# Differential-attention norm of a two-layer decoder: row sums taken with tokens on partitions, then spread back by a product with diagonals

## The reference, cut to what matters

```python
o_b = causal_block_attention(qd, kd, vd, 1.0 / math.sqrt(DIFF_HD),
                             lambda p: p[:, :, 0] - lam * p[:, :, 1])
o_b = rms_norm(o_b, diff_subln_g) * (1.0 - lambda_init)      # over the 128 channels of a head
y_b = o_b.transpose(0, 2, 1, 3).reshape(bsz, s, DIFF_HEADS * DIFF_VD) @ w_out_diff
```

## Time and profile before

| what | value |
|---|---|
| time, median of 3 runs | 1041.09 us (1040.82 to 1041.31) |
| profiled execution | 1040.82 us, of which 1039.0 us from first to last instruction |
| PE matrix products busy | 986.8 us, 95% of the span |
| DVE busy | 741.0 us, 71% |
| ACT busy | 525.2 us, 51% |
| mean granted clock of TensorE | 0.989 of full |

### The profile page before, as it was taken

One profiled execution on the slowest core, in us unless ns is written; L12 is line 12 of the kernel. 1 busy time (PEld: TensorE's weight loads), 2 busy tenths in 40 slices (PEclk: granted clock), 3 DMA queues, 4 the chain that ended last, 5 costly groups with the idle time before them and its releaser, 6 DMA issues.

```text
span 1039.0 us, 20424 instructions
## 1 busy us (share of the span) xinstructions
PE 986.8 (95%) x7817; PEld 917.9 (88%) x7817; DVE 741.0 (71%) x1113; ACT 525.2 (51%) x735; POOL 18.0 (2%) x23
## 2 busy tenths in 40 slices
PE   3699999999999999999999999999999999999997
PEld 2498899889888999989898999888998989999997
DVE  2448889986485787876345698999558577888733
ACT  2655355547444555653345544654734465555532
POOL 5000000000000000000000000000000000000001
PEclk9899999999999999999999999999999999999999
DMA  9865545546594555966763545553678635555551
GB/s 306 293 203 166 174 149 187 173 139 233 203 353 153 161 164 176 350 244 238 275 203 93 161 138 172 187 165 132 204 243 310 216 124 163 177 188 163 185 181 42
DMA packets 138952, 202.25 MB, mean 195 GB/s; under 512 B 3416, under 2 KB 114148, under 8 KB 138852
## 3 DMA queue, kind: packets, MB, share of 16 engines
q1 hardware_dynamic: 138501, 200.68, 57.6%
q10 hardware_dynamic: 351, 0.21, 0.1%
HBM read 199.83 MB, written 1.05 MB: 193 GB/s over the span
## 4 chain that ended last, share of the span: by engine, by line
PE 73%; DVE 13%; issue 7%; ACT 2%; DMA 2%; SPq 2%; DVEq 0%; ACTq 0%
PE PB L1282 16%; PE PB L1284 15%; PE PB L1283 15%; DVE wL L866 5%; DVE buf L953 2%; PE SC L1282 2%; PE MI L1233 2%; PE SC L1283 2%; PE SC L1284 2%; DMA raw<-in_w_in 2%; DVE rdev L1011 1%; PE PB L1305 1%; PE ST L1335 1%; DVE cb L1099 1%; PE TR L1284 1%
## 5 line engine op out<-in xcount | busy, mean ns | idle before, releaser
L866 DVE TENSOR_TENSOR wL<-raw,wH 128x2048 fp32r<-128x2048 f32 (+3 forms) x152 | 322.8, 2125 | 120.1 <-ACT wH L610 118.5
L1282 PE MATMUL PB<-hH,wH 128*128 128x256 f32 x1376 | 398.0, 289 | 7.6 <-DVE wL L866 7.5
L1284 PE MATMUL PB<-hH,wL 128*128 128x256 f32 x1376 | 390.6, 284 | 0.0
L1283 PE MATMUL PB<-hL,wH 128*128 128x256 f32 x1376 | 390.5, 284 | 0.0
L610 ACT ACTIVATE wH<-raw 128x2048 fp32r<-128x2048 f32 (+3 forms) x152 | 268.3, 1782 | 123.9 <-DMA raw<-in_w_down 57.4
L1282 PEld LDWEIGHTS PB<-hH,wH 128*128 128x128 f32 x1376 | 265.1, 193 | 22.7 <-issue 12.3
L1283 PEld LDWEIGHTS PB<-hL,wH 128*128 128x128 f32 x1376 | 265.2, 193 | 0.9 <-issue 0.7
L1284 PEld LDWEIGHTS PB<-hH,wL 128*128 128x128 f32 x1376 | 265.1, 193 | 0.0
L953 DVE SCALAR_TENSOR_TENSOR buf<-G,vec,buf 128x256 f32<-128x256 f32 x240 | 98.0, 477 | 0.3
L1305 PE MATMUL PB<-hH,wH 128*128 128x256 f32 x192 | 56.9, 297 | 15.2 <-DVE hL L883 12.3
L1099 DVE SCALAR_TENSOR_TENSOR cb<-PB,vec,cb 128x255 f32<-128x255 f32 (+1 forms) x88 | 36.3, 476 | 32.2 <-ACT cb L757 32.2
(11 more groups left out here) (257 smaller groups left out, 1695.6 us busy)
## 6 DMA issues: line engine op xcount, KB each, us to landing
raw<-in_w_in SPq DMA_DIRECT2D x48, 1024.0 KB, 5.4
raw<-in_w_up SPq DMA_DIRECT2D x44, 1024.0 KB, 5.1
ada<-in_ada_w SPq DMA_DIRECT2D x40, 1024.0 KB, 7.6
raw<-in_w_down SPq DMA_DIRECT2D x22, 1024.0 KB, 4.9
ada_pre<-in_ada_w SPq DMA_DIRECT2D x8, 1024.0 KB, 11.8
raw<-in_w_o SPq DMA_DIRECT2D x8, 1024.0 KB, 8.3
raw<-in_w_out_diff SPq DMA_DIRECT2D x4, 1024.0 KB, 5.0
raw<-in_w_out_conv SPq DMA_DIRECT2D x4, 1024.0 KB, 7.4
```

The source lines that it names most:

```text
L866: dve.tensor_tensor(wL[s][:, 0:size], raw[s][:, 0:size], wH[s][:, 0:size].bitcast(F32), ALU.subtract).then_inc(w_lo[s], 1)
L1282: pe.matmul(out, a, xh(k), start=first and k == 0, stop=False, skip_group_check=True)
L1283: pe.matmul(out, a, xl(k), start=False, stop=False, skip_group_check=True)
L1284: ins = pe.matmul(out, b, xh(k), start=False, stop=last and k == kt - 1, skip_group_check=True)
```

## The change

The sums of squares are taken with the roles of the operands exchanged: the squares are the stationary operand (four blocks of 128 channels x 128 tokens), two columns of ones the moving one. The result has tokens on partitions and only 8 columns in `ST`, in 4 pairs of equal columns. Root (ACT) and reciprocal (DVE) work on 8 columns in a new tile `rtok`. DVE then multiplies the identity, repeated four times, by the four columns, which gives four 128 x 128 diagonal matrices in `rdev`; PE multiplies ones with these 512 columns (`SPREAD0` behind chunk 18, `SPREAD1` behind chunk 23), and the product has the reciprocal roots in all partitions. The scaling of `oB` reads it straight from the bank and stands one step later than before (19 and 24), as do `oBH` (ACT, 20 and 25) and `oBL` (DVE, 21 and 26). The other uses of `ST` only have their counts moved by two.

```diff
-ST_USES = ["N1", "LAT", "SUB0", "SUB1", "LNS", "LNQ", "N2"]
+ST_USES = ["N1", "LAT", "SUB0", "SPREAD0", "SUB1", "SPREAD1", "LNS", "LNQ", "N2"]
-STATS_AT = {3: "LAT", 17: "SUB0", 22: "SUB1", 26: "LNS", 28: "LNQ"}
+STATS_AT = {3: "LAT", 17: "SUB0", 18: "SPREAD0", 22: "SUB1", 23: "SPREAD1", 26: "LNS", 28: "LNQ"}
...
+        rtok = sb("rtok", [P, 8])
...
                 elif use in ("SUB0", "SUB1"):
                     st_done(l, use)
-                    act.activation(rdev[:, :], ST[:, :], ACT.Sqrt, bias=eps[:, :], scale=1.0 / P).then_inc(st_read, 1)
+                    act.activation(rtok[:, :], ST[:, 0:8], ACT.Sqrt, bias=eps[:, :], scale=1.0 / P).then_inc(st_read, 1)
...
-                if n in (19, 24):
-                    i = (19, 24).index(n)
-                    act.wait_ge(sub_y, l * 2 + i + 1)
+                if n in (20, 25):
+                    i = (20, 25).index(n)
+                    act.wait_ge(st_read, FREE + l * len(ST_USES) + 4 + 2 * i)
                     act.activation(oBH[:, 2 * i:2 * i + 2, :].rearrange("p k t -> p (k t)"),
                                    oBq[:, 2 * i:2 * i + 2, :].rearrange("p k t -> p (k t)"), ACT.Copy).then_inc(sub_hi, 1)
...
                 if n in (18, 23):
 
                     i = (18, 23).index(n)
-                    dve.wait_ge(st_read, FREE + l * len(ST_USES) + 3 + i)
-                    link(dve.reciprocal(rdev[:, :], rdev[:, :]))
+                    dve.wait_ge(st_read, FREE + l * len(ST_USES) + 3 + 2 * i)
+                    link(dve.reciprocal(rtok[:, :], rtok[:, :]))
+                    dve.tensor_tensor(rdev[:, :].rearrange("p (j t) -> p j t", j=4),
+                                      ident.unsqueeze(1).broadcast_to([P, 4, P]),
+                                      rtok[:, 0:8:2].unsqueeze(2).broadcast_to([P, 4, P]), ALU.mult).then_inc(sub_diag, 1)
+                if n in (19, 24):
+                    i = (19, 24).index(n)
+                    dve.wait_ge(st_full, l * len(ST_USES) + 4 + 2 * i)
                     dve.scalar_tensor_tensor(flat(oBq[:, 2 * i:2 * i + 2, :]), flat(oB[:, 2 * i:2 * i + 2, :]), sub_g[:, :],
-                                             rdev[:, :], ALU.mult, ALU.mult).then_inc(sub_y, 1)
-                if n in (20, 25):
-                    i = (20, 25).index(n)
+                                             ST[:, :], ALU.mult, ALU.mult).then_inc(st_read, 1)
+                if n in (21, 26):
+                    i = (21, 26).index(n)
                     dve.wait_ge(sub_hi, l * 2 + i + 1)
...
                 elif use in ("SUB0", "SUB1"):
                     i = int(use[3])
                     after(ob_read, FREE + l * len(OB_USES) + OB_USES.index(("PD1", "PD3")[i]) + 1)
-                    sums = None
+                    free(l, st_read, ST_USES, use)
+                    for j in range(4):
+                        h, a = 2 * i + j // 2, j % 2
+                        ins = pe.matmul(ST[:, 2 * j:2 * j + 2], oBq[:, h, a * P:(a + 1) * P], ones[:, 0:2], start=True,
+                                        stop=True, skip_group_check=True)
+                    ins.then_inc(st_full, 1)
+                    return
+                elif use in ("SPREAD0", "SPREAD1"):
+                    after(sub_diag, l * 2 + int(use[6]) + 1)
+                    free(l, st_read, ST_USES, use)
+                    pe.matmul(ST[:, :], ones[:, :], rdev[:, :], start=True, stop=True).then_inc(st_full, 1)
+                    return
...
-                if sums is None:
-                    pe.matmul(ST[:, :], ones[:, :], oBq[:, 2 * i:2 * i + 2, :].rearrange("p k t -> p (k t)"), start=True,
-                              stop=True).then_inc(st_full, 1)
-                    return
```

More of the change, by code:

```diff
@@ L371, in trunk_kernel @@
         roped, nb_ready, w_ready = sem("roped"), sem("nb_ready"), sem("w_ready")
-        o_hi, sub_y, sub_hi, sub_lo = sem("o_hi"), sem("sub_y"), sem("sub_hi"), sem("sub_lo")
+        sub_diag = sem("sub_diag")
+        o_hi, sub_hi, sub_lo = sem("o_hi"), sem("sub_hi"), sem("sub_lo")
         conv_done, cen_ready, cen_sq, ln_y, ln_t, ln_u, ln_hi, ln_lo = (
@@ L872, in norm @@
             def norm(l, which):
-                dve.wait_ge(st_read, FREE + l * len(ST_USES) + (1, 7)[which])
+                dve.wait_ge(st_read, FREE + l * len(ST_USES) + (1, 9)[which])
                 link(dve.reciprocal(rdev[:, 0:T], rdev[:, 0:T]))
@@ L1021, in mixer_step @@
                 if n == 26:
-                    dve.wait_ge(st_full, l * len(ST_USES) + 5)
+                    dve.wait_ge(st_full, l * len(ST_USES) + 7)
                     dve.tensor_scalar(rdev[:, 0:T], ST[:, 0:T], -1.0 / CONV_CH, None, ALU.mult).then_inc(st_read, 1)
-                    dve.wait_ge(st_read, FREE + l * len(ST_USES) + 5)
+                    dve.wait_ge(st_read, FREE + l * len(ST_USES) + 7)
                     dve.wait_ge(conv_done, l + 1)
@@ L1031, in mixer_step @@
                 if n == 29:
-                    dve.wait_ge(st_read, FREE + l * len(ST_USES) + 6)
+                    dve.wait_ge(st_read, FREE + l * len(ST_USES) + 8)
                     link(dve.reciprocal(rdev[:, 0:T], rdev[:, 0:T]))
```

## The result

The changed kernel took 1051.27 us (median of 4 runs, 1049.12 to 1052.76) against 1041.2 us; the ratio is 1.0095, 95% interval 1.0074 to 1.0117. It is slower, by 10 us. The profiled execution took 1052.46 us, span 1050.7 us. Its runs spread over 3.6 us where those of the kernel before spread over 0.7; the two at 1052.5 and 1052.8 us had a mean granted clock of 0.976, the two at 1049.1 and 1050.1 us of 0.983 and 0.985.

The account below looks back on a forecast made before the run. PE bounds the kernel overall, DVE the norm's stretch; PE's waits for diagonals, clock falls and spreads, less old waits regained, cost 6.2 us per layer, 12.4 in all, giving 1053.5 us, range 1046 to 1057.

Parts of the forecast that it names:

- First wait 2.4 us, second 3.8 us: PE idle before the spreads in steps 18 and 23, waiting for DVE's diagonals: 2.4 us, then 3.8 us.
- DVE loses its lead to `oAH`: In step 19 DVE idles for ACT's `oAH`, behind PE's late values; 3.2 us in hand becomes 3.4 us late.
- Without the clock the loss is 6.2 - 3.0 = 3.2 us per layer: Each layer ends 6.2 us late from the two waits, spreads and clock falls, less the old waits regained.
- A fall of the clock costs 1.5 us, 3 us per layer: Clock falls to 0.50 behind both spread waits, 1.5 us each, priced from chunk 26 against chunk 19.
- Nothing outside the stretch changes: After the second pair PE is nearly always the path and nothing gives time back; 2 x 6.2 = 12.4 us.
- The clock is a case by itself (0.18 and 0.08 for falling less): Clock falls only behind the longer wait: 1050.5 us, chance 0.18; holds both times: 1047.5 us, 0.08.
- The faster rival, 1035.3 us, decided by diagonals ready when PE asks: DVE's relief counts, no waits for diagonals: -2.9 us per layer, 1035.3 us; chance 0.07.
- DVE is the fuller engine from 150 to 222 us: In the first layer's convolution taps and changed norm, DVE is busy 9.96 of 10 us and has no slack.

Follow-up runs that it names:

- experiments 1 and 2: 1: changed kernel with both spreads one step later, 1029.19 us. 2: changed kernel with spreads reading identity copies, not waiting for the diagonals, 1030.68 us.
- experiment 8: Changed kernel with DVE making reciprocal and diagonals ahead of the low half of chunk n + 2 in steps 18 and 23; 1045.34 us.
- Experiment 4: Changed kernel with DVE's taps in steps 19 and 24 ahead of the head pair's half that waits for ACT; 1045.81 us.
- experiment 5: Kernel before the change plus one unused tile of 32 bytes per partition where the changed kernel has rtok; 1037.37 us.
- experiment 7: Changed kernel with only the second spread and its scaling one step later; the first spread still waits in step 18; 1037.48 us.
- experiment 3: Changed kernel with PE's waits filled by useless 512-column products, 3 ahead of the first spread and 5 ahead of the second; 1044.36 us.

## Why the prediction was right

I forecast 1053.5 us and slower; it came to 1051.27, inside the range. Step by step:

- *First wait 2.4 us, second 3.8 us.* Measured 2.56 and 4.13 in both layers. The mechanism (DVE's step 18 starts behind PE's request, and a queue in order keeps all behind it) is shown by experiments 1 and 2, and the wait follows DVE's order to 0.6 us in experiment 8.
- *DVE loses its lead to `oAH`.* Shown in the profile (7.6 and 7.1 us idle, I had said about 5). Experiment 4 adds that one reordering brings back only 0.85 us of the second wait, so the lead couldn't have been kept by it.
- *Without the clock the loss is 6.2 - 3.0 = 3.2 us per layer* (the sum with its two falls of 1.5 us taken out). The filled wait measured 3.6.
- *A fall of the clock costs 1.5 us, 3 us per layer.* Mis-sized: 5.4 us in the first layer, 3.4 in the second. I took the price from one fall whose whole length lay over one row of products and didn't ask how long a fall can last. It lasted 3.4 us in the second layer and 6.8 or 6.9 in the first. In layer 1 of the changed kernel the clock went down while PE still waited; in its layer 2, and at the waits of experiments 4 and 8, it went down only when PE was at work again, and came back after 3.4 us.
- *Nothing outside the stretch changes.* This step failed. The new tile moved its neighbours and speeded up products elsewhere; experiment 5 shows it for 3.8 us. The missed price of the clock (2.4 and 0.4 us more than 3 in the two layers) and this missed gain have opposite signs. In the profiled execution the two stretches cost 16.0 us where I had 12.4, and all the rest gave back 4.3 where I had nothing. The close hit of the total is luck to that extent; the stretches alone, with nothing given back, would have led to about 1057 us, the edge of the range.
- *The clock is a case by itself (0.18 and 0.08 for falling less).* It was right to keep these apart. The same kernel ran from 1049.1 to 1052.8 us with its mean clock, and behind a wait of the same 2.56 us the clock held in the profiled execution of experiment 7 and in layer 1 of experiment 4.
- *The faster rival, 1035.3 us, decided by diagonals ready when PE asks.* Not what the change did, but exactly what the later spread does: its stretch is 49.9 us where the rival's sum, 53.5 - 2.9, gives 50.6. The rule of the Trainium skill, "Perfetto Trace Analysis", section "Optimization Strategies" (relieve the engine that blocks), pays 3.6 us per layer once no new wait is made with it.
- *DVE is the fuller engine from 150 to 222 us.* It is, 71.4 us busy against PE's 68.8, but the row I gave for it, 170 to 180 us, has PE at 10.00 and DVE at 9.96. The argument didn't hang on it.

What stays open: what decides whether the clock falls behind a wait of 2 to 2.6 us and for how long; and which relation of addresses makes products start closer, and by what mechanism.

## What to carry to other kernels

When an operation that had slack is replaced by a chain that goes back through a busy engine, look first at where in that engine's queue the new request stands against the time its operand is ready; the arithmetic saved comes second. The same edit was 10 us slower or 12 us faster than before, by whether PE asked for the diagonals in the step in which DVE makes them or one step later (14 slower or 8 faster, against the old kernel with the new tile's address). And before a few us are credited to a change that allocates a tile, run the old kernel with the tile and without the change.

## What the runs showed of the hardware

- Idle time of PE and its clock: behind 1.91 and 1.92 us (kernel before) and 1.96 us (experiment 8, both layers) the clock fell to 0.50; behind 2.56 us it fell in the changed kernel and held in experiment 7, both layers each, and in experiment 4 it held in the first layer and fell in the second, within one execution. Between the layers it fell behind 2.15 us (kernel before) and held behind 2.10 us (changed). The length of the wait alone doesn't decide. The Trainium skill, "TensorE: Matmul & The Clock Gate", section "HAM oscillation — how this bites in real kernels", says that waits between bursts can throttle the next burst; the trace agrees, and experiment 3 puts 7 us (medians, 1051.3 against 1044.4) to 9 us (the two stretches together) on it here.
- Start-to-start time of products of 128x256: from 0.120 down to 0.117 us, all at granted clock 1.00, by where 32 unused bytes lay. The same page, section "Wait — 56ns, not 53.3ns?", gives N / 2.4 GHz + 2.5 ns for products back to back; worked out for 256 columns, 0.109 us is an estimate from the page, and no run here came to it (here each product has a weight load of its own, 7817 and 7817 in the earlier trace rows).
- DVE's reciprocal costs 3.35 us for 512 columns and 0.20 us for 8; reading one operand from a bank cost nothing (0.73 us, before 0.75 from SBUF).
